# An SSD stage on one core: four passes become one pipeline over 40 blocks, and GpSimd's products move to VectorE and into biases

## What is computed

```
X = x * dt;  a = dt * A;  a_cs = cumsum(a, within a chunk)
decay = exp(where(mask, a_cs[l] - a_cs[s], -inf))        # a 128 x 128 matrix per head and chunk
y_diag = einsum(C B^T * decay, X)
states = einsum(B, exp(a_cs[-1] - a_cs), X)              # one per chunk
prev = scan over the chunks: prev * exp(a_cs[-1]) + states
y_off = einsum(C, prev, exp(a_cs))
```

## Time and profile before

| | |
|---|---|
| three timed runs | 5117.1, 5112.27, 5102.13 us; median 5112.27 |
| profiled execution | 5102.14 us, its span 5100.5 us |
| mean granted clock of TensorE | 0.940 |
| busy share of the span | PE 88%, DVE 70%, POOL 43%, ACT 30% |

### The profile page before, as it was taken

One profiled execution on the slowest core, in us unless ns is written; L12 is line 12 of the kernel. 1 busy time (PEld: TensorE's weight loads), 2 busy tenths in 40 slices (PEclk: granted clock), 3 DMA queues, 4 the chain that ended last, 5 costly groups with the idle time before them and its releaser, 6 DMA issues. The chain is left out here.

```text
span 5100.5 us, 68987 instructions
## 1 busy us (share of the span) xinstructions
PE 4503.8 (88%) x23172; PEld 3705.3 (73%) x23172; DVE 3584.1 (70%) x7429; ACT 1533.9 (30%) x2729; POOL 2199.5 (43%) x1840
## 2 busy tenths in 40 slices
PE   7999999355599979988739599999999999999999
PEld 6888888344344448766538488998998899988888
DVE  3000000687567842269979599999999999999999
ACT  3111100355467742112139422222222222222221
POOL 4222210355334411115467355555555555555554
PEclk9999999676799989999869799999999999999999
DMA  4222221100321134311018899999999899999998
GB/s 137 84 83 83 83 67 39 58 22 30 113 87 50 59 110 153 101 38 42 26 49 231 264 347 333 338 340 334 335 337 339 322 335 337 339 336 332 328 338 295
DMA packets 376377, 978.51 MB, mean 192 GB/s; under 512 B 31096, under 2 KB 155800, under 8 KB 375960
## 3 DMA queue, kind: packets, MB, share of 16 engines
q0 software_dynamic: 156416, 575.12, 30.9%
q1 hardware_dynamic: 218688, 397.83, 23.1%
q10 hardware_dynamic: 1152, 4.19, 0.2%
HBM read 858.96 MB, written 116.75 MB: 191 GB/s over the span
## 5 line engine op out<-in xcount | busy, mean ns | idle before, releaser
L2368 PE MATMUL e_ph<-e_x,e_u 128*128 128x384 f32 x6144 | 1202.5, 337 | 63.5 <-DVE e_x L2433 52.4
L2368 PEld LDWEIGHTS e_ph<-e_x,e_u 128*128 128x128 f32 x6144 | 1096.7, 189 | 137.4 <-issue 47.9
L2390 PE MATMUL e_po<-e_v,e_w 128*128 128x512 f32 x3840 | 996.4, 395 | 22.4 <-DVE e_v L2466 12.5
L2348 POOL DMA_INDIRECT e_row<-in_v_exp,expert_tok x512 | 610.4, 1192 | 478.8 <-DVE e_tok L2493 425.4
L2390 PEld LDWEIGHTS e_po<-e_v,e_w 128*128 128x128 f32 x3840 | 710.8, 188 | 141.9 <-issue 15.2
L2348 POOL DMA_INDIRECT e_row<-in_u_rows,expert_tok x512 | 592.1, 1156 | 477.7 <-DVE e_row L2482 431.3
L324 PE MATMUL proj_acc<-xn,w_tile 128*128 128x512 f32 (+1 forms) x3456 | 677.5, 358 | 4.9 <-POOL w_tile L354 4.9
L2493 DVE SCALAR_TENSOR_TENSOR e_tok<-e_row,e_slot,e_tok 128x1024 f32<-128x1024 f32 x512 | 653.6, 1282 | 9.1 <-DMA e_tok<-h_tok_dram 9.1
L324 PEld LDWEIGHTS proj_acc<-xn,w_tile 128*128 128x128 f32 x3456 | 574.8, 188 | 107.4 <-POOL w_tile L354 5.1
L2482 DVE SCALAR_TENSOR_TENSOR e_row<-e_row,e_tok 128x1024 f32<-128x1024 f32 x512 | 620.8, 1217 | 7.0 <-DMA e_row<-in_u_rows,expert_tok 6.9
L284 DVE COPY proj_out<-proj_acc 128x1280 f32<-128x1280 f32 x25 | 37.3, 1492 | 659.1 <-PE proj_acc L324 646.5
(11 more groups left out here) (314 smaller groups left out, 6723.3 us busy)
## 6 DMA issues: line engine op xcount, KB each, us to landing
e_u_raw<-in_u_exp SPq DMA_DIRECT2D x128, 512.0 KB, 6.6
e_v_raw<-in_v_exp SPq DMA_DIRECT2D x128, 512.0 KB
gates_dram<-g_out SPq DMA_DIRECT2D x6, 8192.0 KB, 30.3
e_g<-gates_dram SPq DMA_DIRECT2D x128, 384.0 KB, 6.6
feat_dram<-proj_out POOLq DMA_DIRECT2D x50, 640.0 KB, 5.8
w_raw<-in_w_feat SPq DMA_DIRECT2D x50, 512.0 KB, 4.9
raw<-feat_dram SPq DMA_DIRECT2D x22, 640.0 KB, 6.2
mx_gate<-feat_dram SPq DMA_DIRECT2D x16, 640.0 KB, 4.0
```

The source lines that it names most:

```text
L2348: pool.indirect_dma_start(out=row[r % RB][:], out_offset=None, in_=u_rows if r < TOK_ROWS else v_rows, in_offset=bass.IndirectOffsetOnAxis ...
L2368: ins = nc.tensor.matmul(ph[q % 2][:, 0:tn], u[b][j][:, kk, :], xs[m][:, kk, t0:t0 + tn], start=(i == 0), stop=(i == 3 * DC - 1))
L2390: ins = nc.tensor.matmul(out, w[b][j][:, blk * P:(blk + 1) * P], v[2 * odd + b][m][:, half * HALF:(half + 1) * HALF], start=(n == 0 and (f ...
```

## The change

There are no passes any more: all loops are unrolled, and one pipeline runs over 40 blocks. While the blocks of a quad run, x of the next quad is activated (at block 3), turned (two tiles a block in blocks 4 to 8) and scanned (blocks 5 to 9 and the first two of the next quad), and the taps of the quad after that are made (blocks 4 to 12). `x_tok`, `prev`, `xT` and `zT` are there twice. The sums keep two pairs of banks; the third pair serves the turns (one bank) and the states (one bank) of quads 1 to 3. The logarithm of dt is added to `ncs`, so that the exponentials bring dt with them, and VectorE makes the product of `ecs` with C. GpSimd keeps the weighing of x.

```diff
+    SILU_AT = 3
+    TURNS_AT = {4 + j: (2 * j, 2 * j + 1) for j in range(TB // 2)}
+    TAPS_AT = {4: (0,), 5: (1,), 6: (2,), 7: (3,), 8: (4,), 9: (5,), 10: (6,), 11: (7, 8), 12: (9,)}
+    STEPS_AT = {5: (0,), 6: (1,), 7: (2,), 8: (3,), 9: (4, 5), 10: (6,), 11: (7,)}
+    def ahead(table, n):
+        q, at = divmod(n, TB)
+        return [(q + 1, i) for i in table.get(at, ())] + [(q, i) for i in table.get(at + TB, ()) if q]
...
# GpSimd
-                pool.memset(prev[:], 0.0)
+                for b in range(2):
+                    pool.memset(prev[b][:], 0.0)
                 pool.memset(zero[:], 0.0).then_inc(masks, 1)
...
-                        pool.wait_ge(ecs_done, n + 1)
-                        nc.gpsimd.tensor_tensor(ecs[ch % EB][:], ecs[ch % EB][:],
-                                                cdup[...].broadcast_to([P, 4, P]), ALU.mult).then_inc(ce_done, 1)
-                        for d in range(2):
-                            pool.wait_ge(exp_done, 2 * n + d + 1)
-                            ins = nc.gpsimd.tensor_tensor(e[ch % EB][d][:], e[ch % EB][d][:], dt[...], ALU.mult)
...
+                for n in range(LAST):
+                    for qn, k in ahead(STEPS_AT, n):
+                        if qn < QUADS:
+                            weigh(qn, k)
# ScalarE
+                act.wait_ge(dve_a, 5)
+                nc.scalar.activation(tmp[1][:], tmp[2][:], ACT.Ln).then_inc(act_a, 1)
...
+                for n in range(LAST):
+                    q, at = divmod(n, TB)
+                    exp_sums(n)
+                    if n:
+                        exp_decays(n - 1)
+                    if at == SILU_AT:
+                        silu_z(q)
+                        if q + 1 < QUADS:
+                            act.wait_ge(y_read, q * TB)
+                            silu_x(q + 1)
+                    for qn, i in ahead(TURNS_AT, n):
+                        if qn < QUADS:
+                            act.wait_ge(y_done, (qn - 1) * TB)
+                            keep_turned(qn, i)
# TensorE
+                def turn_x(q, i):
+                    if q:
+                        pe.wait_ge(x_tok_done, q * TB + i)
...
+                def cumulate(n):
+                    if n >= 2:
+                        pe.wait_ge(masked, n - 1)
...
+                def states(q, k):
+                    pe.wait_ge(xw_done, q * NS + k + 1)
+                    if q:
+                        pe.wait_ge(scanned, q * NS + k)
...
+                for n in range(2, LAST + 3):
+                    if n < LAST:
+                        cumulate(n)
+                    turns = [(qn, i) for qn, i in ahead(TURNS_AT, n) if qn < QUADS]
+                    for qn, i in turns[:1]:
+                        pe.wait_ge(silu_done, 2 * (qn + 1))
+                        turn_x(qn, i)
+                    if n >= 3:
+                        outputs(n - 3)
+                    for qn, i in turns[1:]:
+                        turn_x(qn, i)
+                    for qn, k in ahead(STEPS_AT, n):
+                        if qn < QUADS:
+                            states(qn, k)
# VectorE
+                nc.vector.tensor_scalar(tf[2], dt[:], 2e-38, None, ALU.max)
...
-                    nc.vector.tensor_scalar(ncs_f[:, d, :], seg[0][d]..., -1.0, None, ALU.mult).then_inc(dve_a, 1)
+                    nc.vector.scalar_tensor_tensor(out=ncs[:, d], in0=seg[0][d]..., scalar=-1.0,
+                        in1=tmp[1][:, :, 16 * d:16 * d + 16], op0=ALU.mult, op1=ALU.add).then_inc(dve_a, 1)
...
+                def add_mask(n):
+                    dve.wait_ge(ecs_done, n + 1)
...
+                def matrix(n):
+                    nc.vector.tensor_tensor(ecs[n % EB][:], ecs[n % EB][:], cdup[...].broadcast_to([P, 4, P]),
+                                            ALU.mult).then_inc(ce_done, 1)
+                    m = e[n % EB][0][:]
+                    dve.wait_ge(exp_done, n + 1)
+                    dq.link(nc.vector.tensor_tensor(m, m, e[n % EB][1][:], ALU.add))
+                    nc.vector.tensor_tensor(m, m, cbT[...].broadcast_to([P, 4, P]), ALU.mult).then_inc(m_done, 1)
...
+                for k in range(NS):
+                    decay(0, k)
+                    tap(1, k)
+                    advance(0, k)
+                    if k in EARLY:
+                        add_mask(EARLY.index(k))
...
+                for n in range(LAST + 3):
+                    if len(EARLY) <= n < LAST:
+                        add_mask(n)
+                    scans = [(qn, k) for qn, k in ahead(STEPS_AT, n) if qn < QUADS]
+                    for qn, k in scans[:1]:
+                        decay(qn, k)
+                    for qn, i in ahead(TAPS_AT, n):
+                        if qn + 1 < QUADS:
+                            tap(qn + 1, i)
+                    for qn, k in scans[:1]:
+                        advance(qn, k)
+                    if 0 < n <= LAST:
+                        matrix(n - 1)
+                    for qn, k in scans[1:]:
+                        decay(qn, k)
+                    if n >= 3:
+                        add_skip(n - 3)
+                    for qn, k in scans[1:]:
+                        advance(qn, k)
+                    if n % TB == 2 and n > TB:
+                        gate_quad(n // TB - 1)
```

## The result

The changed kernel takes 5072.66 us (median of four runs, 5070.0 to 5076.07), the kernel before beside it 5109.58 (four runs): ratio 0.9932, 95% interval 0.9914 to 0.995. The profiled execution after is 5070.86 us, its span 5069.3, its mean clock 0.943. The prediction named 5086 us against an earlier median of 5112.3, 26 us less; against the kernel beside it the change brings 36.9.

What follows compares the result with a forecast made beforehand. The scan half is latency, the block half VectorE. 1025.0 + 3 x 78.5, less 0.6, plus 24.6 and 7.8 ends the quads at 1292.3 instead of 1318.5: 26 us less, 5086 us, range 5060 to 5108.

Steps and rivals of the forecast that it cites:

- VectorE's rates and the ports: VectorE's block products: `ecs` 0.72 us, the other two 0.83 and 0.72; GpSimd sharing SBUF ports stretches two-SBUF operations.
- The stretch left beside the weighings: VectorE's loss beside GpSimd's 64 remaining weighings: some 10 us, in proportion to 47 us lost before, of which 6 show.
- Rival 3: SBUF ports as exclusive lock: weighings cost about 16 us in all, leaving 10 us less than before, 5102; chance 0.09.
- First scan: Start up to block 4 of quad 0: first `advance` at 977.5, eight steps, scan done 1009.7, VectorE stands until 1025.0.
- The second clear: Setup: clearing a second `prev` ahead of SP's loads of B and C delays the first convolution by 2.2 us.
- The round: Blocks 4 to 8: sums, exponentials, copy, second turn, states, next sums take 7.5 us; five rounds 38.7 us.
- rival 2: TensorE's low clock in half of the five rounds: a quad is 84.5 us, 8 us less in all, 5104; chance 0.11.
- (a): Block 3 of a quad: ScalarE's exponentials, z, x and tables delay block 4's mask; 13.0 us from block 2's start.
- -0.6: The last quad has no x to activate, which takes 0.6 us off its 78.5.
- wrong if the gates are under 74 us apart: Sign against the forecast: quad gates should be some 78 us apart; under 74 or over 84 would refute it.
- The last six blocks: Last quad's end, with neither taps nor scans: 6 x 4.1 = 24.6 us.
- Rival 1: VectorE alone sets the pace, rounds hide as ScalarE and TensorE run ahead: quad 72.2, 45 us less, 5068; chance 0.16.

Runs made afterwards that it cites:

- 3: Changed kernel with the product of `ecs` with C put back on GpSimd: 5084.62 us, ratio to the kernel before 0.9964.
- 4: Changed kernel with ScalarE making the first turned copy of a block ahead of the eight exponentials: 5046.18 us, ratio to the kernel before 0.9881.
- 5: Changed kernel with the silu of z moved from block 3 to block 9: 5072.32 us, ratio to the kernel before 0.9918.
- 7: Changed kernel with the first turned copy ahead of the exponentials and the `ecs` product back on GpSimd: 5056.43 us, ratio to the kernel before 0.9883.
- experiment 1: Kernel before, its four passes kept, with ln(dt) in the biases and GpSimd's products with dt removed: 5080.43 us, ratio to the kernel before 0.9952.

## Why the prediction came out as it did

**Total.** 26 us less were forecast for the stage, 34.4 came, within the forecast's own 16 to 38. The forecast's end of the quads, 1292.3, becomes 1294.5 in this execution, whose stage began 2.2 us later; it was 1286.30.

**VectorE's rates and the ports: right, a little high.** The `ecs` product was taken at 0.72 us, it is 0.693 on the mean; 0.83 and 0.72 were taken for the other two, which are 0.715 and 0.706. The forecast's figures were distances between starts, and by these the three are shorter still in the last blocks: 0.60, 0.72 and 0.61 (from 1253.01 on). The stretch left beside the weighings was taken at 10 us. Against the unstretched durations it is about 7: (487 - 430) x 64 = 3.6, 59 ns over the three products x 40 = 2.4, 1 in the taps. Rival 3, by which much more of each weighing is paid, set it 16 us above the forecast; that is not there. The 47 us lost before leave out the taps, which fell from 1682 to 1583 ns on the mean, 3 us more.

**First scan: right.** The sums of block 4 were to be done by 1025.0; they ended at 1025.87, that is 1023.7 without the shift. The second clear was taken at 2.2 us. The first convolution comes 12.8 us after the first DMA instead of 11.2, 1.6 later; in kernels 3, 4, 5 and 7, with the same clears, it comes after 13.3 or 13.4, so 2.2 is about right.

**The round: right in mechanism, in size partly by luck.** Five rounds were taken at 38.7 us; quads 1 and 2 show 39.6 (masks from 1107.18 to 1146.75, and from 1185.73 to 1225.35), quad 0 42.3. The rest of a quad was taken at 39.8 and is 39.0 from block 9 of quad 1 to block 4 of quad 2. In each quad the first two rounds begin with eight sums in 1.92 and 2.07 or 2.08 us, the low level of the earlier trace rows, and the fifth ends with eight in 1.91 or 1.92. So the condition of rival 2, the low level in half of the rounds, roughly came about where the forecast had one such round; its price did not. In quad 1 the two low rounds took 8.27 and 8.75 us and the fastest high one 7.16. The forecast had 7.5, and the rival's terms add 2.55 for a low round; the states of the second round stayed at 0.65. More low rounds and shorter high ones thus cancelled to within 0.9 us of the 38.7 in quads 1 and 2, and not in quad 0, where most of the sums are at the low level. Experiment 4 shows that the round was what VectorE stood for.

**The third quad: mis-sized.** "With (a)'s 13.0 a quad is 78.5 us", times three, was the step that failed, and the largest miss. The taps of the last two quads are made while quads 0 and 1 run (`TAPS_AT` goes to the quad after next), so the blocks of quad 2 have none: VectorE is busy 55.3 us there instead of 68.9. Blocks 4 to 8 are no faster for it, as the round sets them; the rest of the quad is, and the gate comes after 71.0. That is 7.5 us by the gates. From the mask of block 4 to that of the next quad it is 69.7 us, 8.2 less than the 77.9 that the forecast comes to for this quad with its -0.6. The mark "wrong if the gates are under 74 us apart" was crossed by this one distance.

**The last six blocks** are 3.8 us each (masks from 1251.81 to 1274.37) where 4.1 was taken, 2 us less, as VectorE's starts are closer than taken; what comes behind them is 0.5 longer. Counted from mask of block 4 to mask of block 4, the deviations are -1.3 at the start, +2.8 in quad 0, none in quad 1, -8.2 in quad 2 and -1.6 at the end: together the 8 us.

**Rival 1** (VectorE alone, 45 us less) is what the same pipeline does once the copy has moved: 58.7 less. The condition named for it, that the rounds hide, was the right one.

**What the forecast did not see** is which part brings the gain. It set the stretch that goes against the rounds that come, and both are there; but by the stage ln(dt) alone brings 31.0 of the 34.4 us, and the pipeline, the largest part of the edit, 6.7 with the product on VectorE and -7.9 (a loss) with it on GpSimd.

## What to carry to other kernels

When two in-order queues hand a buffer to and fro, walk the round once: the shortest instruction in it (here a copy of 0.38 us behind exponentials of 2.44) can set the pace of all others; here its place in the queue was worth more (24.3 us) than the pipeline around it (6.7). Busy time that an engine loses beside another one's work is worth summing over all lines before anything is moved: where the engine was the bound it came back nearly whole (experiment 1), and where others stood close behind it, 10 us less of its work brought nothing (experiment 7). And count work quad by quad, not for an average one: a steady-state term was off by some 8 us because one quad has no taps.

## What the runs showed of the hardware

The stretch goes both ways. GpSimd's 64 weighings, the same instructions in every kernel, take 663 ns on the mean before, where they lie in the scans, 759 after and 872 with the copy first, where VectorE is busy 84% of the stage instead of 79%. By and large, the fuller VectorE, the slower GpSimd; but in 3 they take 758 with VectorE at 72%, beside GpSimd's own other products.

With `ecs` on GpSimd (3) TensorE stayed at the low level for half of the sums or more in rounds in which the changed kernel reached the high one, though the matmuls and their order are the same. The runs don't show why.
